# Hybrid layer of a two-model kernel: one program for three engines in place of eight staged phases

## The reference, cut to what matters

```
fq, fk, fv, ff, gqkv, ga, gb, gz = split(h @ w_in)       # 28 column blocks of 128 and 16 small columns
o_fox = forgetting_attention(fq, fk, fv, cumsum(log_sigmoid(ff + b)))      # 8 heads of 64
gq, gk, gv = split(silu(conv4(gqkv))); q, k = l2norm(gq), l2norm(gk)        # 4 heads of 128
g = cumsum(-exp(a_log) * softplus(ga + dt)); beta = sigmoid(gb)             # cumsum restarts at a chunk
# per chunk: lower = strict(beta k k^T * decay), sol = (1 + lower)^-1 [beta v, beta k e^g]
#            attn = causal(q k^T * decay)
# over the chunks, in order:
u = u_base - w @ S
o = (q e^g) @ S + attn @ u
S = S * e^g_last + k_dec^T @ u
o_gdn = rms_norm(o) * gain * silu(gz)
h = h + concat(o_fox, o_gdn) @ w_out
```

## Time and profile before

| | |
|---|---|
| median of 3 runs | 2166.48 us (2159.18 to 2168.35) |
| profiled execution | 2161.22 us, of which the span from first to last instruction is 2159.4 us |
| TensorE (PE) | 1963.0 us busy, 91% |
| VectorE (DVE) | 1241.5 us busy, 57% |
| ScalarE (ACT) | 1045.8 us busy, 48% |
| GpSimdE (POOL) | 29.5 us busy, 1% |
| mean granted clock of TensorE | 0.944 of 2.4 GHz |
| the part from the first product of mix_in to the last sum of mix_out | 872.5 to 1189.7 us |

### The profile page before, as it was taken

How to read it: one execution, slowest core, us unless ns; L and a number is a source line. 1 busy time by engine, 2 the same in 40 slices (tenths; PEclk the granted TensorE clock), 3 DMA queues, 4 the chain that set the end, 5 groups by cost and what they waited for, 6 DMA issues and landing times. The chain is left out here.

```text
span 2159.4 us, 46047 instructions
## 1 busy us (share of the span) xinstructions
PE 1963.0 (91%) x17620; PEld 1859.8 (86%) x17620; DVE 1241.5 (57%) x2449; ACT 1045.8 (48%) x2015; POOL 29.5 (1%) x24
## 2 busy tenths in 40 slices
PE   5999998999988999896697899989998978978998
PEld 5989998989978999884586899989996878868998
DVE  5667675667665554555433555455547665555554
ACT  4556645456645554443412555455544733245553
POOL 0110000100000000000000000000000000000000
PEclk8999999999999999997676999999998999989999
DMA  6444544444543555331001355545562220014553
GB/s 227 157 137 145 169 159 137 154 137 148 170 152 117 175 175 176 124 110 40 0 1 60 123 171 174 175 132 171 175 224 87 80 78 4 4 55 131 186 187 123
DMA packets 75902, 277.90 MB, mean 129 GB/s; under 512 B 8704, under 2 KB 9984, under 8 KB 75136
## 3 DMA queue, kind: packets, MB, share of 16 engines
q1 hardware_dynamic: 75776, 276.10, 38.9%
HBM read 275.00 MB, written 1.05 MB: 128 GB/s over the span
## 5 line engine op out<-in xcount | busy, mean ns | idle before, releaser
L377 ACT ACTIVATE weights_high<-weight_ring 128x512 fp32r<-128x512 f32 x1016 | 636.3, 631 | 741.2 <-PE psum L406 738.8
L385 DVE TENSOR_TENSOR weights_low<-weight_ring,weights_high 128x512 fp32r<-128x512 f32 x1016 | 688.8, 692 | 497.7 <-ACT weights_high L377 487.7
L404 PE MATMUL psum<-ffn_normed_high,weights_high 128*128 128x272 f32 (+1 forms) x1408 | 407.2, 289 | 21.6 <-DVE ffn_normed_low L423 21.6
L405 PE MATMUL psum<-ffn_normed_low,weights_high 128*128 128x272 f32 (+1 forms) x1408 | 408.2, 290 | 0.0
L406 PE MATMUL psum<-ffn_normed_high,weights_low 128*128 128x272 f32 (+1 forms) x1408 | 407.0, 289 | 0.0
L404 PE MATMUL psum<-first_normed_high,weights_high 128*128 128x256 f32 x1216 | 355.5, 292 | 29.7 <-DVE first_normed_low L423 17.6
L405 PE MATMUL psum<-first_normed_low,weights_high 128*128 128x256 f32 x1216 | 342.0, 281 | 0.0
L406 PE MATMUL psum<-first_normed_high,weights_low 128*128 128x256 f32 x1216 | 341.9, 281 | 0.0
L404 PEld LDWEIGHTS psum<-ffn_normed_high,weights_high 128*128 128x128 f32 x1408 | 269.1, 191 | 23.2 <-issue 23.2
L404 PEld LDWEIGHTS psum<-first_normed_high,weights_high 128*128 128x128 f32 x1216 | 233.8, 192 | 44.8 <-issue 26.5
L406 PEld LDWEIGHTS psum<-ffn_normed_high,weights_low 128*128 128x128 f32 x1408 | 268.9, 191 | 0.0
(11 more groups left out here) (412 smaller groups left out, 2922.0 us busy)
## 6 DMA issues: line engine op xcount, KB each, us to landing
weight_ring<-weights_in SPq DMA_DIRECT2D x508, 512.0 KB, 3.4
arena<-first_in SPq DMA_DIRECT2D x1, 2176.0 KB, 14.1
consts<-const_in SPq DMA_DIRECT2D x1, 1787.5 KB, 17.9
arena<-vec_in SPq DMA_DIRECT2D x1, 1536.0 KB, 9.4
arena<-vec_in SPq DMA_DIRECT2D x1, 1152.0 KB, 6.0
residual<-x_in SPq DMA_DIRECT2D x1, 1088.0 KB, 5.0
out<-normed SPq DMA_DIRECT2D x4, 256.0 KB, 2.2
vectors<-vec_in SPq DMA_DIRECT2D x1, 399.0 KB, 6.5
```

Source lines behind the costliest of these rows:

```text
L377: nc.scalar.activation(WH[:, n % SPLIT, half], W[:, n % RING, half], ACT.Copy).then_inc(weights_high, 1)
L385: nc.vector.tensor_tensor(WL[:, n % SPLIT, half], W[:, n % RING, half], WH[:, n % SPLIT, half].bitcast(F32), ALU.subtract).then_inc(weight ...
L404: nc.tensor.matmul(psum, WH[:, s, cols], high, start=start, stop=False)
L405: nc.tensor.matmul(psum, WH[:, s, cols], low, start=False, stop=False)
```

## The change

The stages 1 to 7 become one order per engine without `end_stage` and without the small transfers and memsets. Chunks are now 16, 64, 64, 64 and 64 positions. The blocks of mix_in come in another order (k, q, v and gate of the delta rule first, then the values and the queries and keys of the attention). All 28 outputs are copied by ScalarE. Between the blocks, TensorE gets the preparation, the Gram matrices, the turns and four of five levels of the inverse (`pe_hybrid_in`); ScalarE and VectorE run the matching steps (`act_hybrid_in`, `dve_hybrid_in`). The inverse works on 20 tiles of 64 by 64 (ten items with two halves). It updates both the inverse `DX` and its transpose `DXT` with products (`pe_delta_ax`, `pe_delta_xax`), so there is no transpose per level. After the last block, `pe_hybrid` alternates the attention's units with the scan's steps. `UN` holds one head half per slot with zeros in the other, so `pe_delta_o` and `pe_delta_state` use 128 rows. Mixer outputs are split as they come. Both output projections begin with the first halves of blocks 0 and 1 (`MIX_ORDER`), and each residual chunk is signalled to the norm. The `end_stage` in front of that norm is gone too. The constants' tensor becomes 82 columns wider.

Removed (heads only) and added (the core):

```diff
-        def pe_project(pe, key, job, high, low, n, part=(0, None)):
-
...
-        def pe_hybrid_in(pe):
+            "in_taken", "small_ready", "z_ready", "log_steps", "rows_ready", "spread", "spread_taken",
+            "exponents", "exponentials", "fox_rows", "convolved", "squares", "sums", "sums_taken",
+            "root", "normed", "values_silu", "grams", "grams_masked", "turned", "turned_taken")}
+        dl = {k: sem("delta_" + k) for k in (
...
+        MIX_ORDER = [(0, 0), (1, 0), (0, 1), (1, 1)] + [(u, h) for u in range(2, KC) for h in range(2)]
+
+        def pe_mix_out(pe, l, job, high, low, n, base):
+            block, _ = BLOCKS["mix_out", l]
+            for u, h in MIX_ORDER:
+                if h == 0:
+                    pe_arrived(pe, block + u)
+                    if u >= 4:
+                        pe.wait_ge(residual_ready, base + u - 4 + 1)
+                for k in range(4 * h, 4 * h + 4):
+                    if u == 0:
+                        pe.wait_ge(act_low, KC * JOBS[job] + (KC if h and l == 0 else k + 1))
+                    mm = pe_tile(PS[:, u % 4, 0:n], block + u, k, high[:, k], low[:, k], k == 0, k == KC - 1)
+                mm.then_inc(blocks_done if h else blocks_half, 1)
...
+        def pe_hybrid_block(pe, i):
+            block, _ = BLOCKS["mix_in", 0]
+            pe_arrived(pe, block + i)
+            if i >= HYB_BANKS:
+                pe.wait_ge(hs["in_taken"], i - HYB_BANKS + 1)
+            for k in range(KC):
+                if i == 0:
+                    pe.wait_ge(act_low, KC * JOBS["hybrid", 0] + k + 1)
+                mm = pe_tile(PS[:, i % HYB_BANKS, 0:S2], block + i, k, MIX_H[:, k], MIX_L[:, k], k == 0, k == KC - 1)
+                if k == KC // 2 - 1:
+                    mm.then_inc(blocks_half, 1)
+            mm.then_inc(blocks_done, 1)
...
+        def pe_decays(pe):
+            pe.wait_ge(hs["spread_taken"], 2)
...
+        def pe_sums(pe, g):
+            pe.wait_ge(hs["squares"], 4 * g + 4)
+            if g:
+                pe.wait_ge(hs["sums_taken"], 1)
+            else:
+                pe.wait_ge(hs["fox_rows"], 5)
...
+        def inv_tiles(g, part, left, right):
+            m0, n = INV_GROUPS[g]
+            for m in range(m0, m0 + n):
+                for o in range(2):
+                    mm = nc.tensor.matmul(inv_psum(g, part)[half(o), m - m0], left[half(o), m], right[half(o), m], start=True, stop=True)
+            return mm
+
+        def pe_delta_flip(pe):
+            pe.wait_ge(hs["grams_masked"], 1)
+            for g in range(3):
+                inv_tiles(g, 0, DU, const("ident_half").unsqueeze(1).broadcast_to([P, ITEMS, TC])).then_inc(dl["ax_ready"], 1)
+
+        def pe_delta_ax(pe, i):
+            for g in range(3):
+                pe.wait_ge(dl["x_new"], 3 * i + g + 1)
+                inv_tiles(g, 0, DU, DX).then_inc(dl["ax_ready"], 1)
+
+        def pe_delta_xax(pe, i):
+            for g in range(3):
+                pe.wait_ge(dl["ax_taken"], 3 * i + g + 1)
+                if i < len(LEVELS) - 1:
+                    inv_tiles(g, 0, DXT, DY)
+                inv_tiles(g, 1, DY, DXT).then_inc(dl["xax_ready"], 1)
...
+        def pe_delta_o(pe, c):
+            w = R_WIDTHS[c]
+            pe.wait_ge(dl["u_taken"], c + 1)
+            if c:
+                pe.wait_ge(dl["o_root"], c)
+            else:
...
+        def pe_hybrid_in(pe, normed):
+            for i in range(HYB_CH):
+                pe_hybrid_block(pe, i)
+                if i == 2:
+                    pe_small(pe, normed)
+                if i == 6:
+                    pe_rows(pe)
+                if i == 7:
+                    pe_decays(pe)
+                if i == 8:
+                    pe_fox_rows(pe)
+                if i == 12:
+                    pe_sums(pe, 0)
+                if i == 14:
+                    pe_sums(pe, 1)
+                if i == 16:
+                    pe_delta_grams(pe)
+                if i == 17:
+                    pe_turn_items(pe, 0)
+                    pe_turn_items(pe, 1)
+                if i == 18:
+                    pe_delta_flip(pe)
+                if i == 19:
+                    pe_turn_items(pe, 2)
+                    pe_delta_ax(pe, 0)
+                if i == 20:
+                    pe_turn_items(pe, 3)
+                    pe_delta_xax(pe, 0)
+                if i == 21:
+                    pe_turn_items(pe, 4)
+                    pe_delta_ax(pe, 1)
+                if i == 22:
+                    pe_turn_items(pe, 5)
+                    pe_turn_items(pe, 6)
+                    pe_delta_xax(pe, 1)
+                if i == 23:
+                    pe_turn_items(pe, 7)
+                    pe_delta_ax(pe, 2)
+                if i == 24:
+                    pe_turn_items(pe, 8)
+                    pe_delta_xax(pe, 2)
+                if i == 25:
+                    pe_delta_ax(pe, 3)
+                if i == 26:
+                    pe_fox_scores(pe, "tail", 0)
+                    pe_delta_xax(pe, 3)
+
+        def pe_hybrid(pe):
+            pe_delta_ax(pe, 4)
+            pe.wait_ge(hs["in_taken"], HYB_CH)
+            pe_fox_scores(pe, "tail", 1)
+            pe_fox_turn(pe, "tail", 0)
+            pe_fox_scores(pe, "pair", 0)
+            pe_delta_xax(pe, 4)
+            pe_fox_scores(pe, "pair", 1)
+            pe_fox_turn(pe, "tail", 1)
+            pe_delta_w(pe)
+            pe_delta_u(pe, 0)
+            pe_fox_turn(pe, "pair", 0)
+            pe_delta_state(pe, 0)
+            pe_delta_u(pe, 1)
+            pe_fox_scores(pe, "pair", 2)
+            pe_delta_o(pe, 0)
+            pe_fox_weigh(pe, 0)
+            pe_delta_state(pe, 1)
+            pe_fox_turn(pe, "pair", 1)
+            pe_delta_sum(pe, 0)
+            pe_delta_u(pe, 2)
+            pe_delta_o(pe, 1)
+            pe_fox_scores(pe, "pair", 3)
+            pe_fox_weigh(pe, 1)
+            pe_delta_state(pe, 2)
+            pe_delta_sum(pe, 1)
+            pe_delta_u(pe, 3)
+            pe_fox_turn(pe, "pair", 2)
+            pe_delta_o(pe, 2)
+            pe_delta_state(pe, 3)
+            pe_fox_weigh(pe, 2)
+            pe_delta_sum(pe, 2)
+            pe_delta_u(pe, 4)
+            pe_fox_turn(pe, "pair", 3)
+            pe_delta_o(pe, 3)
+            pe_delta_sum(pe, 3)
+            pe_delta_o(pe, 4)
+            pe_fox_weigh(pe, 3)
+            pe_delta_sum(pe, 4)
...
+        def act_hybrid_in(act):
+            block, _ = BLOCKS["mix_in", 0]
+            for i in range(HYB_CH):
+                act_split(act, block + i + SPLIT)
+                act.wait_ge(blocks_done, block + i + 1)
...
+                if i == 7:
+                    act.wait_ge(hs["spread"], 1)
+                    nc.scalar.activation(GC_P, PS[:, 3:5, 0:S2], ACT.Copy).then_inc(hs["spread_taken"], 1)
+                    act.wait_ge(hs["spread"], 2)
+                    nc.scalar.activation(BETA_P, PS[:, 5:7, 0:S2], ACT.Exp).then_inc(hs["spread_taken"], 1)
+                if i == 8:
+                    act.wait_ge(hs["spread"], 4)
+                    nc.scalar.activation(EGC, PS[:, 3:7, 0:S2], ACT.Exp).then_inc(hs["spread_taken"], 1)
+                    act.wait_ge(hs["exponents"], 1)
+                    nc.scalar.activation(SC[:, 0:3], SC[:, 0:3], ACT.Exp).then_inc(hs["exponentials"], 1)
+                if i == 9:
+                    act.wait_ge(hs["exponents"], 2)
+                    nc.scalar.activation(DEC, DEC, ACT.Exp).then_inc(hs["exponentials"], 1)
...
+                        act_silu(act, n)
+                if i == 13:
+                    load_log_exp(act)
+                    act_key_root(act, 0)
+                if i == 15:
+                    act_key_root(act, 1)
+                if i == 16:
+                    act.wait_ge(hs["convolved"], 6)
+                    nc.scalar.activation(CO[:, 8:12], CO[:, 8:12], ACT.Silu).then_inc(hs["values_silu"], 1)
+                    act_chain(nc.scalar.activation(HP[:, GZ:GZ + 4], HP[:, GZ:GZ + 4], ACT.Silu))
+                if i == 17:
+                    load_log_exp(act)
+                if i in (18, 20, 21, 22, 24):
+                    act_turned_items(act, {18: 0, 20: 2, 21: 3, 22: 4, 24: 7}[i])
+                if i in (19, 23, 25):
...
+        def dve_delta_ax(dve, i):
+            for g in range(3):
+                dve.wait_ge(dl["ax_ready"], 3 + 3 * i + g + 1)
+                mask = const("partners_half")[:, (1 + i) * TC:(2 + i) * TC].unsqueeze(1).broadcast_to([P, INV_GROUPS[g][1], TC])
+                nc.vector.tensor_tensor(group(DY, g), inv_psum(g, 0), mask, ALU.mult).then_inc(dl["ax_taken"], 1)
+
+        def dve_delta_xax(dve, i):
+            b = LEVELS[i]
+            for g in range(3):
+                dve.wait_ge(dl["xax_ready"], 3 * i + g + 1)
+                dve.wait_ge(dl["x_new"], 3 * i + g + 1)
+                if i < len(LEVELS) - 1:
+                    x = firsts(group(DX, g), b)
```

(75 more changed lines are left out.)

1095 lines of the change are left out of this document (506 added, 589 removed).

## The result

The changed kernel takes 2096.9 us (median of 4 runs, 2096.6 to 2099.3) where the kernel before, on the same chip, takes 2164.5. The ratio is 0.969, with a 95% interval from 0.967 to 0.972. The forecast was 2095 in a range from 2062 to 2132. The profiled execution took 2097.1 us, its span 2095.3.

A forecast was written before the change was run, and what follows sets the result against it. Between mix_in's blocks and mix_out no engine was the bound for long: chains of steps with drains, slowed by the clock. 2161.2 less 60 us for this stretch through mix_out and 6.4 for the norms gave 2095 us, range 2062 to 2132.

The forecast's parts named there:

- mix_in: inserted work and changes of tile shape: Products put between mix_in's blocks take 42 us at full clock; some 45 changes of tile shape add 4 us.
- mix_in: waits: TensorE waits for ScalarE and VectorE before inserted steps between mix_in's blocks, 28 us in sum.
- mix_in: clock, over before: After two waits of 5 us in mix_in, some 8 us of work run at half rate: 4 us lost.
- tail: waits: Waits in the three engines' orders behind block 27, 10 us in sum.
- tail: clock: Behind block 27 the clock averages 0.75, so 42.5 us of work and 10 of waits take 66 us.
- both norms: Norms behind both mix_out: sums end 3.8 us after the last product, saving 3.2 us each, 6.4 in all.
- The price list: Full-clock prices per product for work inserted in mix_in: 0.48 us for 272 columns, 0.057 per 64x64 tile product.
- Rival one: Full clock in the tail, which takes 52 us, and no clock loss in mix_in: 2072 us; chance 0.18 with shorter waits.
- rival two: Half clock throughout the tail, as in the old scan: 2126 us, counted from 2114 to 2135; chance 0.19.
- The slower rival: Mix_in itself loses the clock to the delta rule's waits: half rate costs 129 us more, 2224 us; chance 0.02.
- In-order queues: Weight splits stand behind inserted steps, so TensorE waits 3 us more per block in 15 steps: 2140 us; chance 0.07.
- Part 2: Tail behind block 27, attention with scan: 42.5 us of work at clock 0.75 plus 10 of waits, 66 us.

The follow-up runs named there:

- e5_before_new_out: Kernel before with only both mix_out changed: chunks signalled one by one, no barrier behind them; 2159.4 us against 2166.6, ratio 0.9967.
- e1_gates_first: Changed kernel with VectorE's convolution behind block 4 moved behind the gate rows of block 5; 2086.7 us, ratio 0.965 to the kernel before.
- e11_masks_first: Changed kernel with VectorE's masks and subtractions of the inverse ahead of the weight split in blocks 20 to 27; 2089.5 us.
- e7_inverse_behind: Changed kernel with the inverse's first four levels behind block 27 instead of between blocks 19 to 27; 2083.6 us.
- e4_serial_tail: Changed kernel with all attention units first and then the whole scan behind block 27, on all three engines; 2098.8 us.
- e2_filled_waits: Changed kernel plus 6, 4 and 4 unread TensorE products in the waits behind blocks 6, 7 and 8; 2082.9 us.
- e3_shifted: Changed kernel with gate rows before convolution 1, pe_decays behind block 8, pe_fox_rows behind block 10, keys' first norm one block earlier; 2080.4 us.
- e6_unpaired_tiles: Changed kernel with the inverse's products ordered all upper halves, then all lower halves of a group; 2102.6 us.

## Why the prediction was right

**The sum.** The forecast was 60 us from mix_in to mix_out and 6.4 from the norms. The new products of mix_out end 1.04 us before the sums, at 1129.63. The old ones end 2.57 before theirs, at 1187.93. So the stretch was (1187.93 - 872.47) - (1129.63 - 874.31) = 60.1 shorter, and the norms 6.3. Mix_in started 1.84 us later than before, which no part of the change explains. That makes 60.1 + 6.3 - 1.8 = 64.6 us, against 64.1 between the two profiled executions; the medians lie 67.6 apart. That the sum hit within 2 us is partly luck: 7 us too little in mix_in and 8 too much in the tail cancelled, as the table shows (us; the measured ones from the windows and the quarter-microsecond sums above).

| term | forecast | measured |
|---|---|---|
| mix_in: inserted work and changes of tile shape | 42 + 4 | 128.3 - 84.7 = 43.6 |
| mix_in: waits | 28 | 171.7 - 147.7 = 24.0 |
| mix_in: clock, over before | 4 | 19.4 - 1.9 = 17.5 |
| tail: work | 42.5 | 45.3 |
| tail: waits | 10 | 7.1 |
| tail: clock | 14 | 6.0 |
| mix_out | 26 | 25.2 |
| both norms | 6.4 saved | 6.3 saved by rows, 7 (4 to 10) by e5_before_new_out |

**Inserted work.** The price list held: 46 against 43.6. TensorE's timeline of the new kernel has the first 16 turns, at full clock, with the next block's product at 978.03:

```profile
976.13 1.97 PE L1523 MATMUL psum<-consts,arena 128*64 128x128 f32 x32
```

That is 0.12 us a product, half of the 0.22 for all 128 rows, so products into 64-row halves do pair. The Gram products took 4.00 / 20 = 0.20 each at a clock that was partly low. A 64x64 product takes 0.060 in a long row (0.057 forecast). With the prices at full clock in the new traces (0.43 for 272 columns, 0.12, 0.060) I estimate the list at 39 us, which leaves some 5 for going in and out of the blocks, where 4 were forecast. The rule of the Trainium skill ("TensorEngine Tiling (Array Packing)", Key Properties) by which a change of tiling mode drains TensorE would have given 5 us more. The trace agrees that a change costs time, 0.3 us in and out around tiles, but the sum has no room for the upper value.

**Waits.** Five of the named ones came as priced or smaller: `pe_rows` 3.17 (4.6), `pe_decays` 2.03 (2.2), `pe_fox_rows` 1.97 (2.2), Grams 4.43 (5.0), first inverse step 2.64 (2.6). The reason given for the first, VectorE behind a convolution, is what e1_gates_first undid. For the inverse I gave the reason too, masks behind VectorE's split, and e11_masks_first confirms it for five of the seven waits between blocks 20 and 27. The two others (1.54 and 1.61) wait for ScalarE. What I did not see is that these waits outweigh what the place between the blocks brings (e7_inverse_behind).

**The clock, the step that was mis-sized.** "After two waits of 5 us I expect some 8 us of work at half rate in all: 4 lost." It was 17.5. The row that I leaned on, 1730 to 1735 with 3.70 us busy of 5 and 1.00, showed only that one loose stretch can keep the clock. Here one wait of 3 us and two of 2, with eight to ten of busy time between them, went with 0.62 over 36 us. In the tail, on the other hand, I took 0.75 from the old attention and the old scan, and it ran at 0.89, with 7.1 us of waits in 58.4. Rival one (full clock in the tail, 2072) and rival two (half clock, 2126) both missed, rival one by less. The 0.14 between 0.75 and 0.89 is just inside the 0.15 that I had named as a sign of being wrong. Had both clocks been forecast right, the sum would have been 2095 + 13.5 - 8 = 2100.

**The slower rival.** Mix_in did lose clock to the delta rule's waits, by the mechanism named, for 17 us and not 129: its mean clock while busy was 128.3 / 147.7 = 0.87, far from the 0.66 at which it would decide.

**In-order queues.** This rival named the right mechanism (work behind a split) with the sign of the price reversed: the blocks hardly wait for late splits, but inserted steps wait behind splits that stand ahead of them in VectorE's order and aren't ready yet. It cost 7 us and not 45.

**The norms.** Two misses cancelled here. The first is a reading of mine: "The last addition of mix_out starts at 1189.2, so its products end at about 1189.15." In the kernel before the last product ends at 1187.93, and VectorE has a split between it and the addition:

```profile
1187.64 0.29 PE L406 MATMUL psum<-mixer_high,weights_low 128*128 128x272 f32 x1
1188.63 0.69 DVE L385 TENSOR_TENSOR weights_low<-weight_ring,weights_high 128x512 fp32r<-128x512 f32 x1 [0.82 <-ACT weights_high L377]
```

The old sums thus ended 8.09 us behind the last product and not 6.9. The second: "With chunks signalled, seven of eight sums are ready" failed. ScalarE's timeline of the new kernel at the end of mix_out:

```profile
1129.67 0.63 ACT L382 ACTIVATE weights_high<-weight_ring 128x512 fp32r<-128x512 f32 x1 [0.82 <-PE psum L411]
1130.21 2.01 ACT L502 ACTIVATE squares<-residual 128x272 f32<-128x272 f32 x6
```

The squares stand behind the split of the next matrix's second block, whose second half ends at 1130.3. So the sums start 1.0 us after the last product and then run at full clock for 3.93. From the end of the last product (1129.63) to the end of the sums it is 4.97 us and not 3.8. Against 8.09 that saves 3.1 where 3.2 was forecast, and at the second norm 7.92 - 4.74 = 3.2.

**Alternation.** Part 2 forecast the tail as a whole and never said what the alternation adds. e4_serial_tail says: about 2 us of its 58. The gain of the tail is that stages, barriers and their gaps went and the clock stayed up.

## What to carry to other kernels

An engine's own program order is a resource: before a step is put between the blocks of a projection, look where its helper operations land in the other engines' queues, and keep them ahead of any instruction that waits for the block (7 us here, with not one instruction added). A chain whose groups overlap by themselves, like this inverse, can stand behind the projection in one piece. Count a short wait of TensorE with the clock that follows it; here three waits of 7 us in sum cost 20, and moving their steps to where the inputs are ready took 16.5 us off.

## What the runs showed of the hardware

- Products that nobody reads made the kernel 14 us faster (e2_filled_waits): with 14 products in three waits the clock stayed at 1.00 from 902 to 938, where without them it was 0.62. Block 7, behind the first wait, then takes 3.30 us in place of 5.09, the difference between the upper level (2.4 GHz) and mostly the lower one (1.2 GHz).
- Which waits bring the clock down isn't a matter of their length alone. Seven waits of 0.7 to 1.8 us between 996 and 1046 went with 1.00 throughout. In e1_gates_first one of 2.03 us was followed by 0.54, although no wait had come before it since mix_in began at 873.7. In e3_shifted the same wait of 1.84 us before L1547 that left 1.00 in the new kernel (1033.80) was followed by 0.59 (1016 to 1019). What separates them stays open.
- Pairs of 64x64 float32 tiles in opposite halves cost 0.064 to 0.069 us per product of 64 columns, one half at a time 0.079 to 0.089 (e6_unpaired_tiles, 40 and 20 products). In one long row the pairs cost 0.060 (e7_inverse_behind).
- Going from a block to 20 such tiles and back costs 0.3 us beside the products (e11_masks_first against e7_inverse_behind).
- What `pe_delta_o` would cost with 64-row halves, and so what a change of tile shape costs within a short chain, wasn't tried.
